# The tokens' norm scales, laid along the columns: through TensorE, or through a DRAM scratch on GpSimd's queue

## What is computed

```
def rmsnorm(x, g, eps=NORM_EPS):
    xf = x.astype(jnp.float32)
    y = xf * lax.rsqrt(jnp.mean(xf * xf, axis=-1, keepdims=True) + eps)
    return (y * g.astype(jnp.float32)).astype(x.dtype)
...
        h = rmsnorm(x, attn_norm[l])
        qkv = jnp.einsum('bsd,de->bse', h, w_qkv[l])
...
        h = rmsnorm(x, ffn_norm[l])
        g = causal_dwconv(jnp.einsum('bsd,df->bsf', h, w_gate[l]), conv_w[l], conv_b[l])
        u = jnp.einsum('bsd,df->bsf', h, w_up[l])
```

## Time and profile before

| what | value |
|---|---|
| median of 3 runs | 2352.54 us (2351.71 to 2352.75) |
| the profiled execution | 2351.49 us, its span 2349.7 us |
| PE busy | 2334.0 us, 99% of the span |
| DVE, ACT busy | 1569.5 us (67%), 1232.6 us (52%) |
| POOL | 4.2 us, 11 instructions |
| granted PE clock | 0.998 of full |
| DMA | 436.20 MB, mean 186 GB/s |

### The profile page before, as it was taken

One profiled execution on the slowest core, in us unless ns is written; L12 is line 12 of the kernel. 1 busy time (PEld: TensorE's weight loads), 2 busy tenths in 40 slices (PEclk: granted clock), 3 DMA queues, 4 the chain that ended last, 5 costly groups with the idle time before them and its releaser, 6 DMA issues.

```text
span 2349.7 us, 31399 instructions
## 1 busy us (share of the span) xinstructions
PE 2334.0 (99%) x12126; PEld 1993.3 (85%) x12126; DVE 1569.5 (67%) x2464; ACT 1232.6 (52%) x1878; POOL 4.2 (0%) x11
## 2 busy tenths in 40 slices
PE   9999999999999999999999999999999999999998
PEld 7888888888888888888888888888888888888887
DVE  6697877777777557755668556666766566566555
ACT  6566666555555445544656555656445345345343
POOL 0000000000000000000000000000000000000000
PEclk9999999999999999999999999999999999999999
DMA  7545444556555555565564545654555655665664
GB/s 290 191 158 176 144 162 164 178 183 204 185 180 201 194 178 201 184 219 190 166 204 155 180 149 167 213 180 152 191 192 183 198 193 182 199 193 182 216 196 152
DMA packets 119300, 436.20 MB, mean 186 GB/s; under 512 B 13392, under 2 KB 13648, under 8 KB 118128
## 3 DMA queue, kind: packets, MB, share of 16 engines
q1 hardware_dynamic: 117792, 426.13, 55.3%
q0 software_dynamic: 928, 7.47, 0.9%
q10 hardware_dynamic: 432, 0.60, 0.1%
HBM read 432.05 MB, written 2.10 MB: 185 GB/s over the span
## 4 chain that ended last, share of the span: by engine, by line
PE 95%; DVE 3%; ACT 1%; issue 1%; DMA 0%; ACTq 0%; DVEq 0%
PE bank L509 29%; PE bank L523 15%; PE bank L491 15%; PE bank L493 15%; PE bank L492 15%; DVE lo_w L1460 1%; PE bank L573 1%; DVE xT L1633 0%; ACT hi_w L992 0%; PE bank L791 0%; PE bank L803 0%; PE bank L615 0%; PE bank L601 0%; PE bank L637 0%; DVE x L1531 0%
## 5 line engine op out<-in xcount | busy, mean ns | idle before, releaser
L1460 DVE TENSOR_TENSOR lo_w<-raw_w,hi_w 128x1024 fp32r<-128x1024 f32 x804 | 964.3, 1218 | 537.9 <-ACT hi_w L992 536.8
L992 ACT ACTIVATE hi_w<-raw_w 128x1024 fp32r<-128x1024 f32 x804 | 833.0, 1052 | 581.6 <-PE bank L493 399.0
L509 PE MATMUL bank<-xT,hi_w 128*128 128x512 f32 x3008 | 721.3, 391 | 2.6 <-ACT hi_w L992 2.6
L509 PEld LDWEIGHTS bank<-xT,hi_w 128*128 128x128 f32 x3008 | 552.9, 188 | 110.0 <-DVE xT L1645 3.3
L523 PEld LDWEIGHTS bank<-xT,lo_w 128*128 128x128 f32 x3008 | 388.4, 191 | 16.2 <-DVE lo_w L1460 0.7
L523 PE MATMUL bank<-xT,lo_w 128*128 128x256 f32 x3008 | 397.4, 284 | 0.5 <-DVE lo_w L1460 0.5
L491 PE MATMUL bank<-hi_w,act_hi 128*128 128x512 f32 x864 | 336.4, 389 | 0.0
L493 PE MATMUL bank<-hi_w,act_lo 128*128 128x512 f32 x864 | 336.1, 389 | 0.0
L492 PE MATMUL bank<-lo_w,act_hi 128*128 128x512 f32 x864 | 336.1, 389 | 0.0
L491 PE MATMUL bank<-hi_w,xT 128*128 128x512 f32 (+1 forms) x672 | 266.0, 396 | 2.1 <-DVE lo_w L1460 1.9
L493 PE MATMUL bank<-hi_w,xT 128*128 128x512 f32 (+1 forms) x672 | 261.6, 389 | 0.0
(11 more groups left out here) (340 smaller groups left out, 1566.2 us busy)
## 6 DMA issues: line engine op xcount, KB each, us to landing
raw_w<-in_w_up SPq DMA_DIRECT2D x216, 512.0 KB, 4.2
raw_w<-in_w_down SPq DMA_DIRECT2D x216, 512.0 KB, 4.0
raw_w<-in_w_gate SPq DMA_DIRECT2D x88, 512.0 KB, 4.2
raw_w<-in_w_in SPq DMA_DIRECT2D x72, 512.0 KB, 3.9
raw_w<-in_w_qk SPq DMA_DIRECT2D x64, 512.0 KB, 4.2
raw_w<-in_w_v SPq DMA_DIRECT2D x32, 512.0 KB, 3.8
raw_w<-in_w_o SPq DMA_DIRECT2D x32, 512.0 KB, 3.5
raw_w<-in_w_out SPq DMA_DIRECT2D x32, 512.0 KB, 3.6
```

The lines of the kernel that those rows point to most:

```text
L509: last = e.matmul(pair[c][:, :], hi_w[:, slot, at:at + P], both[:, kt].rearrange("p h t -> p (h t)"), start=(kt == 0), stop=(kt == g.kts - ...
L992: e.activation(hi_w[:, u % SPLIT_SLOTS, 0:unit_cols[u]], raw_w[:, u % RAW_SLOTS, 0:unit_cols[u]], ACT.Copy).then_inc(s["w_hi"], 1)
L1460: e.tensor_tensor(lo, raw_w[:, u % RAW_SLOTS, 0:unit_cols[u]], hi.bitcast(F32), ALU.subtract).then_inc(s["w_lo"], 1)
```

## The change

Diagonal squares, ones product and copy go, for all five rows. POOL gets a helper of its own: it waits until the scales are there, writes them (256 numbers of 4 bytes) to a DRAM scratch, waits for that transfer, and reads the 1 KB back with a stride of zero over the partitions into the row's tile. Its semaphore `row_landed_<name>` takes the place of `row_copied`. The first row's two DMAs stand ahead of those of `lams` and `rel`. On DVE the first four `times_row` move one unit back.

```
-    "root_pre", "root_sqrt", "root_post", "row_diag", "row_spread", "row_copied", "rowed", ...
+    "root_pre", "root_sqrt", "root_post", "row_out", "rowed", ...
+        row_dram = {name: nc.dram_tensor(f"row_{name}_scales", (TT, P), F32, kind="Internal").ap() for name in ROW}
 # tensor_program
-            def spread_row(name, pairs):
-
-                if pairs:
-                    e.wait_ge(s["turned_lo"], 2 * pairs)
-                e.wait_ge(s["row_diag"], ROW[name] + 1)
-                e.matmul(banks[4][:, 0:TOK], const("ones"), token_rows[name][:, :],
-                         start=True, stop=True).then_inc(s["row_spread"], 1)
             units(9)
+            e.wait_ge(s["ident_landed"], 16)
             e.wait_ge(s["consts_landed"], 16)
-            spread_row("attn", TURNED0["y1"])
             units(3)
...
 # vector_program
             def times_row(stage, tile):
                 out = turned_out(stage, tile)[0]
                 e.wait_ge(s["sum_out"], sum_count[stage, tile])
-                e.wait_ge(s["row_copied"], ROW[ROWED[stage]] + 1)
+                e.wait_ge(s[f"row_landed_{ROWED[stage]}"], 16)
...
             units(5)
             token_scales("attn", 8)
-            diagonal_row("attn", 0)
-            units(3)
-            spread_row("attn")
+            units(4)
             for g in groups[0:2]:
                 for c in range(2):
                     times_row("qk", 2 * g.part + c)
-            units(2)
+            units(1)
             e.wait_ge(s["rel_landed"], 16)
...
             turn_x("ffn", 3)
             units(1)
             token_scales("ffn", 8)
-            diagonal_row("ffn", 0)
             units(3)
-            spread_row("ffn")
...
 # gpsimd_program
+            def spread_row(name, col):
+
+                e.wait_ge(s["root_post"], 4 * (ROOT[name] + 1))
+                e.dma_start(row_dram[name].rearrange("t p -> p t"), stats[:, col:col + TT],
+                            allow_slow_non_contiguous=True).then_inc(s["row_out"], 16)
+                e.wait_ge(s["row_out"], 16 * (ROW[name] + 1))
+                e.dma_start(token_rows[name][:, :], bass.AP(tensor=row_dram[name].tensor, offset=0,
+                                                            ap=[[0, P], [1, TOK]])).then_inc(s[f"row_landed_{name}"], 16)
+
             e.wait_ge(s["consts_landed"], 16)
+            spread_row("attn", 0)
             e.dma_start(lams[:, :, :], bass.AP(tensor=dram["lambdas"].tensor, offset=0,
                                                ap=[[0, P], [HD, 4], [1, HD]])).then_inc(s["lams_landed"], 16)
             e.dma_start(rel[:, :, :], dram["rel"]).then_inc(s["rel_landed"], 16)
+            spread_row("ffn", 0)
...
+            spread_row("mem", 2)
+            spread_row("cross", 0)
+            spread_row("mlp", 0)
```

More of the change, by code:

```diff
@@ L59 @@
     "xT_landed0", "xT_landed1", "xT_landed2", "xT_landed3", "x_landed0", "x_landed1", "warm_cleared", "warmed",
-    "x_hi", "x_lo", "mem_hi", "mem_lo",
+    "x_hi", "x_lo", "mem_hi", "mem_lo", "row_landed_attn", "row_landed_ffn", "row_landed_mem", "row_landed_cross", "row_landed_mlp",
     "raw_landed0", "raw_landed1", "raw_landed2", "raw_landed3",
@@ L63 @@
     "w_hi", "w_lo", "w_used", "part_out", "sum_out", "copied", "x_added", "x_gained", "x_scaled", "x_squared",
-    "root_pre", "root_sqrt", "root_post", "row_diag", "row_spread", "row_copied", "rowed", "rms_squared", "rms_normed", "final_scaled", "final_scaled_dve",
+    "root_pre", "root_sqrt", "root_post", "row_out", "rowed", "rms_squared", "rms_normed", "final_scaled", "final_scaled_dve",
     "turned_pe", "turned_hi", "turned_lo", "tiled_pe", "tiled",
@@ L609, in diff_scores @@
                     e.wait_ge(s["diff_maxed"], 4 * h)
-                else:
-                    e.wait_ge(s["row_copied"], 1)
                 for t in range(TT):
@@ L885, in tensor_program @@
             units(4)
-            spread_row("ffn", TURNED0["mix"])
             units(last_unit["down1_1"] + 1 - done[0])
             units(6)
-            e.wait_ge(s["row_copied"], 2)
             for piece in range(3):
@@ L946, in tensor_program @@
             units(2)
-            spread_row("mem", TURNED0["mlp"])
             units(8)
-            e.wait_ge(s["row_copied"], 3)
-            spread_row("cross", TURNED0["mlp"])
             units(3)
-            e.wait_ge(s["row_copied"], 4)
             head_scores("cross", 0)
@@ L976, in tensor_program @@
             units(4)
-            spread_row("mlp", TURNED0["mlp"] + 8)
             units(n_units - 4 - done[0])
@@ L1509, in turned_group @@
                     e.wait_ge(s["sum_out"], sum_count["up2", 2 * pair + 1])
-                    e.wait_ge(s["row_copied"], ROW["mlp"] + 1)
+                    e.wait_ge(s["row_landed_mlp"], 16)
                     e.tensor_tensor(cv, cv, row_mlp[:, :].unsqueeze(1).to_broadcast([P, 2, TOK]),
@@ L1613, in final_scales @@
                 e.wait_ge(s["root_post"], n + 4)
[L1615 to L1624, removed]
             def turn_lo(burst, gain_name, dst, first, n, dst0=0):
@@ L2075, in vector_program @@
             rms_scales("mem", D, 2)
-            diagonal_row("mem", 2)
             units(2)
@@ L2079, in vector_program @@
             token_scales("cross", 8)
-            diagonal_row("cross", 0)
             units(2)
-            spread_row("mem")
             units(8)
-            spread_row("cross")
             units(3)
@@ L2102, in vector_program @@
             token_scales("mlp", 8)
-            diagonal_row("mlp", 0)
             units(3)
-            spread_row("mlp")
             units(n_units - done[0])
```

## The result

The changed kernel takes 2377.44 us (median of 4 runs, 2375.02 to 2378.49) against 2352.22 us before: a ratio of 1.0108 with a 95% interval of 1.0096 to 1.0120. It is slower by 25 us. The forecast was 2354.1 us with a range up to 2357.4.

A forecast was written before the change was run, and what follows sets the result against it. PE was taken as the bound, busy 2334.0 of 2349.7 us. Row products -1.7, chain +2.0, clock +1.0 and `ffn` +0.3 sum to +1.6 on 2352.54, giving 2354.1 us, range 2350.3 to 2357.4.

The forecast's parts named there:

- The write: POOL's 1 KB write of the first row's scales to DRAM, taken as 2.5 us, with 6.4 at the slow end.
- Rival 2: Slow write (6.4 us) between POOL's write and read delays everything behind it; chain 5.9 late, +6.9, 2359.4 us; chance 13%.
- `ffn`, put at 1.0 at most: Second row: write and read about 7 us against 8.0 until first use; +0.3 taken, up to 1.0 if late.
- `mlp`, put at nothing: Last row: 8.4 us from square to first use and wider margins than `ffn`, so no cost.
- `mem`, put at nothing too: Row first used still later behind its scales than `ffn` and `mlp`, so no cost.
- Rival 3: First row's read alone slow, landing at 42.6; DVE waits for the row, `rel` in time; 2355.8 us; chance 9%.
- Rival 1: Later issue spreads the loads, `rel` lands in time, all five rows pay: 2350.0 to 2351.0 us; chance 20%.
- The chain from `rel` to unit 15: No slack from DVE's first use of `rel` (41.50) to PE at unit 15 (54.54); `rel` late adds +2.0 us.
- the read of 6.4: First row's 1 KB read spread over 128 partitions, taken as 6.4 us like `lams`, landing the row at 38.7.
- `rel`'s 9.8: Load of `rel`, issued about 33.7 instead of 28.75, keeps its old 9.8 us and lands at 43.5.
- The clock: PE's wait at unit 15 grows to 3.0 us, then half clock for a stretch: +1.0, between 0 and 1.7.
- what a row product costs: On PE 0.42 us a row, 2.1 for five; four rows without a PE wait give -1.7.

The follow-up runs named there:

- probe_writes: Kernel before plus ten extra writes to DRAM on GpSimd's queue, with varied piece sizes, counts and spacings, awaited by GpSimd alone: 2353.54 us in one run.
- four_packed: Changed kernel with the first row made by PE again and `lams`, `rel` first; the other four rows by the packed write: 2364.39 us, ratio 1.0059.
- turned_write: Changed kernel, but DVE transposes the scales so each write is 8 pieces of 128 bytes instead of 256 of 4: 2356.18 us, ratio 1.0018.
- turned_rel_first: Changed kernel with DVE's transpose and write of 8 pieces, and `lams` and `rel` issued ahead of the first row's write and read: 2355.36 us, ratio 1.0015.
- probe_spacing: Kernel before plus seven extra writes, five on GpSimd's queue and two on SP's, mostly between packed and 64 bytes apart: 2351.58 us in one run.

## Why the prediction was wrong, point by point

**The write failed.** The step is "I take 2.5, near the quiet end, since almost no data moves". It measured 10.0, 8.9, 10.3, 12.0 and 9.4 us. The nearest rows were 2.0 (`pos`) and 6.4 (`lams`). Neither bounds it. `pos` reads its 128 pieces of 8 bytes out of DRAM in 2.0 us; the same shape written into DRAM took 4.3 (b of probe_writes), and 256 packed pieces of 4 bytes, which is what this writes, 9.0 (a). That is the mis-sized term that all the others hang on: without the writes the kernel is at 0.9992, with writes of 2 us at 1.0018, with the packed ones at 1.0108.

**Rival 2 had the mechanism and the place** ("POOL's wait between write and read", 13%), with 6.4 as its worst and +6.9 for all. At the first row its rule held, a microsecond of PE for each that `rel` is late; there were 10.8 of them instead of 5.9. With the clock behind it this is about the 13 us that four_packed gives to that row. What the sum lacked is the same lateness at the other rows. Write and read need over 16 us there, where DVE has 8.0 at `ffn` and 8.4 at `mlp`. `ffn`, put at 1.0 at most, cost PE 5.8, `mlp`, put at nothing, 4.6, and each was followed by half clock, where one stretch in all was reckoned with. Even `mem`, put at nothing too, cost 1.1: write and read end 16.7 us after the write's issue, and in the kernel before its row was first used 11.4 us behind the square (1540.48 to 1551.93). `mlp` is the place that the text named as one that could go wrong.

**What DVE waits for.** It was said to be `rel` and not the row. It was the row: 11.56 against 1.33. With the write put right (turned_write) DVE waits for both, 3.27 and 3.30. Rival 3 had named the wait at the row, but took its 42.6 for a slow read alone, while the text had worked 42.6 out from a slow write and a slow read together. The measured row lands at 48.3, by the write. Rival 1 speaks of the same queues, but the traces list `lams` and `rel` on POOL's queue and the weights' loads on SP's.

**Right.** The chain from `rel` to unit 15 was right in kind. In turned_write, where write and read have nearly the durations that the sum took, `rel` is 4.2 late (2.0 forecast) and PE waits 4.6 (3.0), so even there the sum is too low: +4.7 us against +1.6, partly because `rel` took 11.2 and not 9.8. Right were also the read of 6.4 (6.5 at the first row) and `rel`'s 9.8 (9.4). The clock fell as forecast: the changed kernel's five waits of 2.4 to 5.8 us behind the rows were followed by stretches at 0.50. Right, too, was what a row product costs, from the timeline of PE in the changed kernel, to be held against the earlier trace rows:

```profile
35.85 2.08 PE L524 MATMUL bank<-xT,lo_w 128*128 128x256 f32 x16
37.76 0.40 PE L510 MATMUL bank<-xT,hi_w 128*128 128x512 f32 x1
```

37.76 - 35.85 = 1.91, the time without a row product, at the place where it was 2.33.

**The rule of the skill.** The Trainium skill, "DMA: Bandwidth & Descriptors", on the anatomy of one DMA on the gpsimd path, gives 2.0 us for 1 KB. The runs agree for single writes of 1 KB whose pieces are 128 bytes and more (1.6 to 2.0 us) or 4 bytes with at least 32 from one to the next (2.1). They do not agree for packed pieces of 4 bytes (9.0), nor where the queue was loaded (6.9 behind `rel` in turned_rel_first). The Trainium skill's rules for kernel authors on the same page, one descriptor per element where the last dimension is not contiguous, were weighed for rival 2. They name the right shape of transfer, but many pieces alone were not slow: 256 of them with gaps took 2.1 us.

## What to carry to other kernels

A small DMA that nobody would call traffic can be the slowest in the kernel: before a scatter of 4-byte pieces into DRAM is put on a path, time it by itself, and put the pieces on whole rows first (here a DVE copy of 0.17 us and a transpose of 0.24 turned 10 us into 2). Bound an operation that the trace does not show by rows of the same direction and granularity, not by rows of the same size; where there are none, leave the range open. And count a detour through DRAM as write plus read (here 16 us, and 7 to 9 with the transpose) against the time until the row is used (8 us). It can pay only where that is clearly longer, and what it could win here was 0.42 us a row.

## What the runs showed of the hardware

- Pieces of 4 bytes written into DRAM, side by side, take 9.0 us for 256 pieces, 8.4 for 128 and 7.0 for 64. With 8, 16 and 32 bytes from one to the next, 256 pieces take 4.3, 3.1 and 2.1, and with 64 or 512 still 2.1 (probe_writes, probe_spacing). Why close pieces hinder each other was not looked into.
- Such a write nearly stops the core's other DMAs: 28 and 32 GB/s flow in all in 7 us of it, where 257 flow beside the same pieces with gaps. The loads of `w_qx`, 512 KB each, that lie beside two such writes in the changed kernel took 9.9 us in the median instead of 3.5. It is so from SP's queue too (31 GB/s).
- A wait of PE of 1.9 us is not always followed by half clock: in the kernel before it was (1.89 at 1528.88), in the changed kernel one of 1.92, which ended at 1550.16, was not, as a window of PE (us, busy, clock, DMA share, GB/s) shows:

```profile
1550.10:1553.50 3.40, 3.34 (x15) 1.00 0.59 187
```
